# The l2 norms of q and k in a delta-rule block: from the data into gate columns and head norm

## What is computed

```python
def l2_norm(x):
    xf = x.astype(jnp.float32)
    return xf * lax.rsqrt(jnp.sum(xf * xf, axis=-1, keepdims=True) + NORM_EPS)
...
        q = l2_norm(q.reshape(bsz, t_len, N_HEADS, HEAD_DIM)) * (HEAD_DIM ** -0.5)
        k = l2_norm(k.reshape(bsz, t_len, N_HEADS, HEAD_DIM))
...
        o_fwd = gated_delta_rule(q, k, v, g[:, :, 0], beta[:, :, 0])
        o_bwd = rev(gated_delta_rule(rev(q), rev(k), rev(v), rev(g[:, :, 1]), rev(beta[:, :, 1])))
        o = rms_norm(o_fwd + o_bwd, delta_norm_g[i]) * jax.nn.silu(z.reshape(bsz, t_len, N_HEADS, HEAD_DIM))
```

## Time and profile before

| what | value |
|---|---|
| median of 3 runs | 2261.77 us |
| lowest and highest run | 2260.52 and 2264.62 us |
| span of the profiled execution | 2263.8 us |
| its own time beside the span | not listed apart; the span is taken for it |
| mean granted clock of TensorE | 0.987 |
| q/k/v stages | 135 to 230 us and 448 to 552 us |
| rounds 0 to 3, 4 to 7 | 230 to 445 us, 552 to 772 us |

### The profile page before, as it was taken

One profiled execution on the slowest core, in us unless ns is written; L12 is line 12 of the kernel. 1 busy time (PEld: TensorE's weight loads), 2 busy tenths in 40 slices (PEclk: granted clock), 3 DMA queues, 4 the chain that ended last, 5 costly groups with the idle time before them and its releaser, 6 DMA issues.

```text
span 2263.8 us, 35147 instructions
## 1 busy us (share of the span) xinstructions
PE 2193.4 (97%) x14360; PEld 1830.8 (81%) x14360; DVE 1281.8 (57%) x1899; ACT 838.7 (37%) x1282; POOL 197.6 (9%) x142
## 2 busy tenths in 40 slices
PE   6999999999999999999999999999999999999998
PEld 5878788788888888888888898888887678888887
DVE  4788899877866455444433454444237835444423
ACT  4355433355455233333322353223233544223222
POOL 0100222200433001000000100000000110000000
PEclk9999999999999999999999989999999999999999
DMA  4232111121111243233332313233321112232321
GB/s 159 77 131 75 48 44 44 53 69 57 49 34 44 90 153 126 93 95 99 107 102 85 116 58 101 93 102 108 102 68 57 47 56 66 93 102 93 110 100 51
DMA packets 56173, 189.90 MB, mean 84 GB/s; under 512 B 6257, under 2 KB 8689, under 8 KB 56049
## 3 DMA queue, kind: packets, MB, share of 16 engines
q1 hardware_dynamic: 53168, 182.88, 25.2%
q10 hardware_dynamic: 2880, 5.24, 0.6%
HBM read 178.66 MB, written 9.44 MB: 83 GB/s over the span
## 4 chain that ended last, share of the span: by engine, by line
PE 81%; issue 10%; DVE 7%; ACT 2%; DMA 0%; POOL 0%; SPq 0%; ACTq 0%; DVEq 0%; POOLq 0%
PE pg L639 68%; PE pC L898 4%; PE pB L898 1%; DVE cpad L1862 1%; DVE w_lo L1782 1%; PE pB L670 1%; DVE sacc L1972 1%; ACT w_hi L1200 1%; PE pC L743 1%; PE pA L952 1%; PE pA L717 0%; PE pB L701 0%; PE pB L677 0%; PE pC L717 0%; DMA xin<-in_x 0%
## 5 line engine op out<-in xcount | busy, mean ns | idle before, releaser
L639 PE MATMUL pg<-a_hi,w_hi 128*128 128x512 f32 (+1 forms) x1920 | 749.2, 390 | 14.3 <-DVE a_lo L1841 3.7
L639 PE MATMUL pg<-a_lo,w_hi 128*128 128x512 f32 (+1 forms) x1920 | 741.0, 386 | 0.0
L639 PE MATMUL pg<-a_hi,w_lo 128*128 128x512 f32 (+1 forms) x1920 | 739.0, 385 | 0.0
L1782 DVE TENSOR_TENSOR w_lo<-w_raw,w_hi 128x1024 fp32r<-128x1024 f32 (+3 forms) x299 | 382.8, 1280 | 412.0 <-ACT w_hi L1200 409.7
L1200 ACT ACTIVATE w_hi<-w_raw 128x1024 fp32r<-128x1024 f32 (+3 forms) x299 | 329.7, 1103 | 652.2 <-PE pg L639 641.2
L639 PEld LDWEIGHTS pg<-a_hi,w_hi 128*128 128x128 f32 x1920 | 363.6, 189 | 88.8 <-issue 8.0
L639 PEld LDWEIGHTS pg<-a_hi,w_lo 128*128 128x128 f32 x1920 | 363.4, 189 | 69.1 <-issue 1.5
L639 PEld LDWEIGHTS pg<-a_lo,w_hi 128*128 128x128 f32 x1920 | 363.6, 189 | 68.3 <-issue 0.9
L639 PE MATMUL pg<-h_hi,w_hi 128*128 128x512 f32 (+1 forms) x572 | 215.7, 377 | 0.6 <-DVE w_lo L1782 0.6
L639 PE MATMUL pg<-h_hi,w_lo 128*128 128x512 f32 (+1 forms) x572 | 214.5, 375 | 0.0
L639 PE MATMUL pg<-h_lo,w_hi 128*128 128x512 f32 (+1 forms) x572 | 212.4, 371 | 0.0
(11 more groups left out here) (355 smaller groups left out, 2430.0 us busy)
## 6 DMA issues: line engine op xcount, KB each, us to landing
w_raw<-in_w_gu SPq DMA_DIRECT2D x132, 512.0 KB, 3.5
w_raw<-in_w_in SPq DMA_DIRECT2D x74, 512.0 KB, 3.5
w_raw<-in_w_dn SPq DMA_DIRECT2D x48, 704.0 KB, 4.0
spill_g<-tmp ACTq DMA_DIRECT2D x16, 256.0 KB, 2.1
w_raw<-in_w_co SPq DMA_DIRECT2D x8, 512.0 KB, 3.6
w_raw<-in_w_do SPq DMA_DIRECT2D x8, 512.0 KB, 3.8
w_raw<-in_w_wo SPq DMA_DIRECT2D x8, 512.0 KB, 4.0
w_raw<-in_w_pg SPq DMA_DIRECT2D x8, 512.0 KB, 3.7
```

Of the source, the lines that this page charges most:

```text
L639: ins = pe.matmul(dst[:, cols], w_of(w, n % 2, k), b(k)[:, cols], start=first and q == 0, stop=last and q == len(todo) - 1)
L1782: dve.tensor_tensor(w_lo[:, n % 2, 0:c], w_raw[:, n % 4, 0:c], w_hi[:, n % 2, 0:c].bitcast(F32), ALU.subtract).then_inc(S("w_lo"), 1)
```

## The change

It drops roots, reciprocals, spreads and products of the l2 norm. SiLU writes q and k straight into `qT` and `kT`. The sums of squares of four heads are kept side by side in PSUM, and behind the last head of a stage `head_factors` makes from them: beta / n_k^2 for the Gram products (new column 6 of `gat`), the same factor on column 3, beta / n_k on column 1, for v, and `qe`, an epsilon per token for the head norm, which `output_means` adds. k is transposed right behind its SiLU, into another bank (`turned`); v of a stage's last head is transposed in the next round behind its Gram products. TAIL is cut in two parts, of 9 and 15 products. QKV_TAPS grows by one tap in both places, and one gap in each of rounds 0 to 3 loses three. Waits on semaphores are renamed to fit; those on `trc` move from the head of a round to its first small product.

```diff
@@ -438,13 +440,13 @@
 
         TAPS = [(t, j) for pair in ((1, 2), (3, 4), (5, 6), (0, 7)) for j in range(CK) for t in pair]
         GLU_TAPS = (5, 6)
-        QKV_TAPS = (4, 2)
+        QKV_TAPS = (5, 3)
 
 
         A_, B_ = 4, 4
         GAP = [16, 17, 4, A_, B_, A_, B_, 1, B_] + [A_, B_] * 2 + [6, 8, 8]
         GAP3 = [14, 14, 2, 3, 3, 3, 3, 1, 3] + [3, 3] * 2 + [4, 5, 5]
-        TAP = [1, 2, 0] + [1, 2] * 2 + [1, 3, 1, 2, 1, 3] + [0, 13, 0]
+        TAP = [1, 2, 0] + [1, 2] * 2 + [1, 3, 1, 2, 1, 3] + [0, 10, 0]
         TAP4 = [1, 2, 0] + [1, 1] * 4 + [1, 2] + [0, 10, 0]
         PD = 4
...
@@ -832,6 +834,22 @@
                     b, c = (nb2, tmps[h % 2]) if h < HH else (nb, osq[h - HH])
                     token_sums(b[:, NC * (h % HH):NC * (h % HH) + NC], (c,)).then_inc(S("ons"), 1)
 
+            def turn_k(h):
+
+                pe.wait_ge(S("silu"), 3 * h + 2)
+                wait(pe, "trc", 2 * h - 1)
+                for c in range(NC):
+                    ins = pe.transpose(turned[:, 0, c * P:(c + 1) * P], kT[:, h % HH, c * P:(c + 1) * P], ident)
+                ins.then_inc(S("trp"), 1)
+
+            def turn_v(h):
+
+                pe.wait_ge(S("silu"), 3 * h + 3)
+                wait(pe, "trc", 2 * h)
+                for c in range(NC):
+                    ins = pe.transpose(turned[:, 1, c * P:(c + 1) * P], sacc[:, h % 2, 2, c * P:(c + 1) * P], ident)
+                ins.then_inc(S("trp"), 1)
+
             def qkv(half):
                 if half:
...
@@ -847,19 +865,13 @@
                     if hh:
                         pe.wait_ge(S("l2sq"), 2 * h)
                         for i in range(2):
-                            ins = token_sums(nb[:, NC * i:NC * i + NC], (sq[:, i, :],))
+                            q = NC * (2 * (hh - 1) + i)
+                            ins = token_sums(nb[:, q:q + NC], (sq[:, i, :],))
                         ins.then_inc(S("l2s"), 1)
                     if hh < HH:
                         unit(("qkv", 3 * h + 1))
                     if h == 0:
                         decay_sums()
-                    if hh == HH:
-                        unit(TAIL[half], part=(9, 18))
-                    if hh:
-                        pe.wait_ge(S("l2i"), h)
-                        wait(pe, "qk_fin", 2 * (h - 1))
-                        for i in range(2):
-                            spread(l2b[:, i], nst[:, 1, NC * i:NC * i + NC]).then_inc(S("l2f"), 1)
                     if half and hh == 0:
                         output_sums(0, 2)
                     if hh < HH:
@@ -870,20 +882,12 @@
                         pe.wait_ge(S("on_r"), 1)
                         wait(pe, "on_g", hh - 1)
                         spread(nb2, ost[:, NC * (hh - 1):NC * hh]).then_inc(S("onf"), 1)
+                    if hh:
+                        turn_k(h - 1)
+                    if 0 < hh < HH:
+                        turn_v(h - 1)
                     if hh == HH:
-                        unit(TAIL[half], part=(18, UNIT))
-                    if hh:
-
-                        pe.wait_ge(S("qk_fin"), 2 * h)
-                        wait(pe, "trc", 2 * (h - 1))
-                        for c in range(NC):
-                            ins = pe.transpose(trb[:, 0, c * P:(c + 1) * P], kT[:, hh - 1, c * P:(c + 1) * P], ident)
-                        ins.then_inc(S("trp"), 1)
-                        pe.wait_ge(S("silu"), 3 * h)
-                        for c in range(NC):
-                            ins = pe.transpose(trb[:, 1, c * P:(c + 1) * P],
-                                               sacc[:, (h - 1) % 2, 2, c * P:(c + 1) * P], ident)
-                        ins.then_inc(S("trp"), 1)
+                        unit(TAIL[half], part=(9, UNIT))
 
             def gap(R, g):
...
@@ -913,11 +917,15 @@
                     g_col = gat[:, 0, c, d * 8 + HH * half + hh:d * 8 + HH * half + hh + 1]
                     ins = pe.matmul(pA[:, j, :], g_col.to_broadcast([P, P]), tri[d], start=True, stop=True)
                 ins.then_inc(S("grow"), 1)
+                if r == 0:
+                    pe.wait_ge(S("l2n"), 3 * (half + 1))
                 for j, d, hh, c in prob:
 
                     tok = slice(c * P, (c + 1) * P)
                     ins = pe.matmul(pB[:, j, :], kT[:, hh, tok], kT[:, hh, tok], start=True, stop=True)
                 ins.then_inc(S("gram"), 1)
+                if r == 0:
+                    turn_v(HH * (half + 1) - 1)
                 gap(R, 0)
                 pe.wait_ge(S("eg"), R + 1)
...
@@ -930,6 +938,8 @@
                     pe.wait_ge(S("ls"), LEVELS * R + lv + 1)
                     if lv == 0:
                         wait(pe, "s_upd", (NC - 1) * half + r)
+                        if r == 0:
+                            pe.wait_ge(S("trc"), 2 * HH * (half + 1))
                         small(c0, ls[:, 0], None).then_inc(S("y"), 1)
                         if R == 5:
...
@@ -1346,6 +1356,11 @@
                 act.wait_ge(S("gD"), 3)
                 act.activation(gat[:, 4], gat[:, 4], ACT.Exp).then_inc(S("g_all"), 1)
 
+            def turned_out(h, i):
+
+                act.wait_ge(S("trp"), 2 * h + i + 1)
+                act.activation((ktok, vtok)[i][:, h % HH], quad(turned[:, i], NC), ACT.Copy).then_inc(S("trc"), 1)
+
             def qkv(half):
                 def padded(h, i):
...
@@ -1360,11 +1375,12 @@
                 def silu(h, i):
                     act.wait_ge(S("stap"), SK * (3 * h + i + 1))
                     y = sacc[:, h % 2, i]
-                    act.activation(y, y, ACT.Silu).then_inc(S("silu"), 1)
+                    dst = (qT[:, h % HH], kT[:, h % HH], y)[i]
+                    act.activation(dst, y, ACT.Silu).then_inc(S("silu"), 1)
                     if i < 2:
                         act.wait_ge(S("silu"), 3 * h + i + 1)
                         wait(act, "l2s", h)
-                        act.activation(sq[:, i, :], y, ACT.Square).then_inc(S("l2sq"), 1)
+                        act.activation(sq[:, i, :], dst, ACT.Square).then_inc(S("l2sq"), 1)
 
                 def head_squares(h0, h1):
...
@@ -1385,24 +1401,11 @@
                         padded(h, 0)
                     if half and hh == 0:
                         head_squares(0, 2)
-                    def l2_root():
-                        act.wait_ge(S("l2s"), h)
-                        for i, s in enumerate((float(P), 1.0)):
-
-                            c = slice(NC * i, NC * i + NC)
-                            ins = act.activation(nst[:, 0, c], nb[:, c], ACT.Sqrt, scale=s, bias=eps_t[:, 1 + i:2 + i])
-                        ins.then_inc(S("l2r"), 1)
-
-                    if hh == HH:
-                        l2_root()
                     if hh:
                         silu(h - 1, 2)
-                    if 0 < hh < HH:
-                        l2_root()
                     if half and hh == 1:
-                        act.wait_ge(S("ons"), HH)
-                        act.activation(ost[:, 0:HH * NC], nb2[:, 0:HH * NC], ACT.Sqrt, scale=1.0 / P,
-                                       bias=eps_t[:, 0:1]).then_inc(S("on_root"), 1)
+                        act.wait_ge(S("on_m"), 1)
+                        act.activation(ost[:, 0:HH * NC], ost[:, 0:HH * NC], ACT.Sqrt).then_inc(S("on_root"), 1)
                     if hh < HH:
                         padded(h, 1)
                         if h == 0:
@@ -1416,9 +1419,11 @@
                         if half and hh == 1:
                             act.wait_ge(S("bv"), 4)
                             act.wait_ge(S("kt"), NC - 1)
-                        for i, dst in enumerate((ktok, vtok)):
-                            act.wait_ge(S("trp"), 2 * (h - 1) + i + 1)
-                            act.activation(dst[:, hh - 1], quad(trb[:, i], NC), ACT.Copy).then_inc(S("trc"), 1)
+                        turned_out(h - 1, 0)
+                        if hh < HH:
+                            turned_out(h - 1, 1)
+                act.wait_ge(S("l2n"), 3 * half + 2)
+                act.activation(kn[:, 1], kn[:, 0], ACT.Sqrt).then_inc(S("kr"), 1)
                 after(TAIL[half])
                 gate_out(TAIL[half])
...
@@ -1944,6 +1950,37 @@
                 dve.tensor_tensor(gat[:, 4], gat[:, 4], gat[:, 2], ALU.subtract).then_inc(S("gD"), 1)
                 dve.tensor_tensor(gat[:, 3], gat[:, 3], gat[:, 1], ALU.mult).then_inc(S("g_k"), 1)
 
+            def output_means(half):
+
+                q = slice(HH * NC * half, HH * NC * (half + 1))
+                dve.wait_ge(S("ons"), HH * (half + 1))
+                dve.scalar_tensor_tensor(ost[:, q], (nb2, nb)[half][:, 0:HH * NC], 1.0 / P, qe[:, q], ALU.mult, ALU.add)\
+                    .then_inc(S("on_m"), 1)
+
+            def head_factors(half):
+
+                dve.wait_ge(S("l2s"), HH * (half + 1))
+                sums = nb[:, 0:2 * HH * NC].rearrange("p (h i c) -> p i c h", h=HH, i=2)
```

(51 more changed lines are left out.)

15 lines of the change are left out of this document (7 added, 8 removed).

## The result

The changed kernel took 2248.79 us (median of 5 runs, 2245.64 to 2249.63) against 2261.77 (5 runs): a ratio of 0.9931 [0.9913, 0.9948], 13.0 us less. Executed again in two later sessions, it took 2244.46 and 2244.38 us: ratios of 0.9904 [0.9884, 0.9925] and 0.992 [0.99, 0.9939]. Over all 17 runs its median is 2245.35 us, that of 71 runs of the kernel before is 2261.59: 16.2 us less, where 20.7 were forecast. The profiled execution has a span of 2247.8 us and took 2249.63 in all, 1.8 us more; by the same 1.8 us that of the kernel before took about 2265.6 (an estimate), 3.8 us above its median and not 2.0.

What follows compares the result with a forecast made beforehand. TensorE was taken as the bound, DVE a close second in the edited stages. 8.0 + 6.7 + 1.6 + 4.4 = 20.7 us off the 2261.77 us median gave 2241.0 us, range 2238 to 2244; about 85% from 2233 to 2249.

Steps and rivals of the forecast that it cites:

- What bounds the kernel: Whole kernel: TensorE, busy 2193.4 of 2263.8 us, is the bound; only work or waits taken off its queue pay.
- The spreads: Both q/k/v stages: each head's spread of 16 PE instructions costs 1.8 us, and eight of them go.
- First stage: First q/k/v stage: fewer spreads and waits on PE make it 8.0 us shorter, of a possible 10.8.
- the rule: ScalarE table loads: skill page puts a switch at about 2.66 us; the forecast used the row's 1.28 us instead.
- Rounds: Rounds 0 to 3: three taps fewer in each shorten PE's waits for DVE's output sums, 6.7 us; bounds 0 and 8.
- The clock at the head of the second stage: Start of second q/k/v stage: a wait of 1.0 us leaves PE at 2.4 GHz, gaining 1.6 us; bounds 0 and 1.6.
- Second stage: Second q/k/v stage: 4.4 us gained despite a 6.1 us PE wait for DVE and low clock; bounds 3.0 and 6.0.
- Carried to the end: From round 4 on: nothing is changed and PE is 97% busy, so the whole gain should last to the end.
- taps without worth: Rounds 0 to 3: PE's wait for outputs only becomes one for masks, 6.7 us go; 2247.7 us, chance 0.10.
- The rival of a worse clock: Second stage: low level also after the shorter wait, and twice as long after the 6.1 us; 2244.2 us, chance 0.20.
- the new root late: First stage: a table switch of twice 1.28 us delays kn's root, rounding and Exp by 1.3 us; 2242.3, chance 0.03.
- DVE late with w_lo inside the stages: Both q/k/v stages: PE waits before each weight unit and drops to 1.2 GHz; 2266 us or more, chance 0.02.

Runs made afterwards that it cites:

- spreads_back: The changed kernel with eight spreads of constants, which nobody reads or waits for, put back on PE in place of the old ones; 2251.09 us, 0.9948.
- taps_last: The changed kernel with the second stage's last tail products ahead of PE's long wait, and three taps behind the head factors in each stage's last head; 2238.9 us.
- before_again: The kernel before the change, word for word, executed again; 2261.54 us, 1.0003.
- busy_half: The changed kernel with 22 dummy products, which nothing reads, ahead of PE's 6.6 us wait at the end of the second stage; 2244.69 us, 0.991.
- tail_first: The changed kernel with the tail unit's last 15 products moved ahead of the wait for the scaled head, in the second stage alone; 2242.99 us, 0.9917.
- old_taps: The changed kernel with its twelve moved taps back where they were before the change; 2251.42 us, 0.9953.

## Why the prediction came out as it did

**What bounds the kernel** (right): PE is at 97% again, and what the cuts gained is work and waits taken off PE.

**The spreads** (right): 1.8 us each; spreads_back closes to 0.4 us in the first stage and 0.1 in the second.

**First stage** (right, 8.2 for 8.0): l2n came at 220.6, not 221.2, Exp at 225.40, not 226.1, the first small product at 232.79, not 233.6, because PE and DVE each ran half a microsecond ahead from the start on; the 8.2 between the cuts is free of that. The wait before the Gram products was 1.20 (0.5 to 1.3), the one for POOL's mask 1.0 (1.5). On the tables the row decides against the rule: the load starts at 219.33 and the root at 220.62, 1.29 us later, although kn's reciprocal came only behind 220.07, and in taps_last the same 1.29 us lie between load and root with the reciprocal long done. By the 2.66 us a switch of the Trainium skill, ScalarE: Activation LUTs, What ACT_TABLE_LOAD costs, the root could not have begun before 222.0; no row here has the drain.

**Rounds** (right in mechanism, the clock's part by luck of the execution): 6.7 + 1.6 forecast, 7.5 measured, 5.7 of it idle time and 1.8 busy time. The four waits for the outputs fell from 8.7 to 2.5 us, so 6.2 and not 6.7, since before the second stage 1.4 remained and not 1.0; 0.5 went into smaller waits. The clock at the head of the second stage stayed up. That term has the right size for one low stretch, but the kernel before has it at that place in only one of two executions; in before_again it comes after round 0, costs 3.1 us of busy time, and the rounds gain 8.8.

**Second stage** (right, 4.3 for 4.4, in the execution shown): the wait was 6.55 us (6.1 to 7), with the low level behind it; busy_half prices that at 1.7 us (1.6). In the other two executions of the kernel after the low level cost 2.8 and 2.7, and the stage gained 3.2 and 3.3 against the execution of before that is shown, near the lower bound of 3.0.

**Carried to the end** (the step that failed, in size): "From round 4 on nothing is changed, and PE is 97% busy, so the gain should be carried to the end." 20.1 us stood at round 4, and 16.0 at the end of the compared spans. It was allowed as 3 us of clock either way, but the same program varied by 12 us there, and the 13.0 us first measured became 16.2 over more runs. The first median, 2248.79, lies 0.2 us inside the wide range to 2249 and outside the one of 2238 to 2244; that the wide one held it is luck, as its upper end came from a rival (taps without worth) that did not come true. The position of the execution was wrong too, 3.8 us above its median and not 2.0, as the page shows no own time; that does not touch the forecast, which is the median less 20.7 either way. The rival of a worse clock, 2244.2, is the nearest to the 2245.35 of all runs. Its second half (a low level lasting twice as long after the long wait) came true in two executions of three, for 1.1 of its 1.6 us; its first half (the low level behind the shorter wait before the second stage) in none.

**The rivals:** the taps buy nothing in the rounds (wrong, they give all 7.5); the new root late (wrong, above); DVE late with w_lo inside the stages (wrong, one wait of 0.7 us as before). What stays open is why the low stretches fall where they do, behind round 4 and after the waits of the rounds, and whether some of the 0.0011 of mean clock belongs to the kernel's own 6.6 us wait: the kernels without it ran at 0.987 to 0.989, which the spread of the runs does not separate.

## What to carry to other kernels

Cut both traces at products that they share, compare length by length, and split each length into idle and busy time: lengths at the full clock repeated to a few hundredths of a microsecond, those with a low stretch in them were up to 1.3 us apart, where medians of the whole could not tell 13 us from 16. Take a second execution of both kernels before a term for the clock is called confirmed. Moving work to a second engine is free only where that engine's chain does not release the first; the same taps were worth 7.6 us with the l2 change and nothing without it. Before sending work behind a wait, look at which engine's chain comes next: three taps moved gave 2 us where they stood ahead of what PE waited for, and none where ACT's chain, which starts ahead of them, came later.

## What was not expected of the hardware

- The same program's length behind round 4 was 1702.4, 1700.4 and 1690.1 us; where the first and the third were compared, the granted clock was 0.01 apart in each stretch.
- 5.16 us of products that nothing reads, put into a 6.6 us wait, kept the clock at 1.00 and made the stage 1.7 us shorter; the 1.51 us of standing still that was left did not lower it, nor did the 3.0 us in tail_first.
- The length of a wait does not settle it. The 3.08 us after round 0 left the level at 1.00 in the execution shown of the kernel before and brought 0.50 in before_again and old_taps; the 2.99 us before the second stage brought it in the kernel before and in old_taps and not in before_again; the 2.20 us behind them brought it in both executions of the kernel before.
